# Second self-attention of a two-block model: 32x32 block transposes on VectorE and a gather by ScalarE's transfers in place of TensorE transposes

## The chip, the cores and the metric

One core of a Trainium2 chip runs the whole program in one launch. The metric is the device time of one execution in microseconds. All matrices are fp32. The large products are made on TensorE as three fp32r products of a high and a low part (high times high, high times low, low times high), so that every weight tile is first rounded to its high part and then has its rest taken.

## What is computed

Two blocks run one after the other on x of 512 tokens by 1024 features, each of two layers. In both layers of the second block one of three branches is a self-attention with 8 query heads and 2 key/value heads of 64 features, over all 512 tokens:

```python
q = rmsnorm(q.reshape(B, L, 8, 64), qn); k = rmsnorm(k.reshape(B, L, 2, 64), kn)
q, k = apply_rope_2(q, cos, sin), apply_rope_2(k, cos, sin)
s = jnp.einsum("bkgqd,bktd->bkgqt", qblk, k) * 64 ** -0.5     # per block of 128 queries
p = jax.nn.softmax(s, axis=-1)
o = jnp.einsum("bkgqt,bktd->bkgqd", p, v)                     # then @ w_br_attn, gated
```

The other two branches of such a layer are a long convolution and a gated linear attention. Their products, the gates' and the branches' output products stand between the pieces of this attention in the program.

## The kernel before

The program is a list of units (`order_of_work`), each a product with its weights or a small step, and every engine walks the same list and takes from each unit its own part. Engines meet through semaphores. So the order of the list is the order of each engine's queue, and an instruction that waits holds up all that stands behind it on its engine. Where several lists of units are merged, a string of digits (`PICKS`) says which list gives the next unit; they were fixed beforehand.

**Weights.** SyncE loads weight tiles of 512 or 256 KB into three raw buffers (`next_raw`, L2542), ScalarE rounds them to the high part (`next_halves`, L1327), GpSimd takes the rest (`next_rest`, L1710), and TensorE multiplies (L929 to L931). There are three split buffers, and the part of tile w + 2 stands in the unit of tile w. A product with 8 slices of 128 rows has 24 matmuls (the units `q`, `gate`, `gvtok`), one with 4 slices has 12 (`by`).

**The attention of a layer** goes over c = 0..3 (pairs of query heads, one pair in each c, hh = 0, 1) and in it over i = 0..3 (128 queries each):

- `sc` (L1098): for hh = 0, 1 a fp32 product of 64x128 queries and 64x512 keys into a score bank. There are three score banks, taken in turn (S0, S1, O).
- VectorE takes the row's maximum of each bank (L2088) and scales it (L2092). ScalarE exponentiates both (L1515), with the sum of each row, from the score banks into PB, which holds two i.
- `tr` (L994): TensorE transposes the eight 128x128 pieces of PB into banks T0 and T1. VectorE copies T0 (L2118) and ScalarE T1 (L1535) into PTB, in which keys lie on partitions.
- VectorE inverts the sums (L2104) and spreads them over VF (L2111).
- `pbc` (L994): four transposes of VF; ScalarE copies them back to VF (L1519).
- `pv` (L1125): after the fourth i, eight fp32 products of V (128x64) with PTB (128x512) into bank O, in two halves of the array. `bsplit` multiplies by VF (L1961) and splits the result for the branch's product (L1447, L1796).

Queries are rotated with eight small transfers on SyncE's queue for each c (QB<-RXB). In a layer `tr` occurs 16 times and `pv` 4 times. Behind the last `pv` the gated linear attention begins: `gfront` (L1213), `gscan` with its exponentials on ScalarE (L1582 to L1586), and `gvtok`, which takes the four banks S0, S1, T0, T1.

```python
score_bank: return (S0, S1)[hh] if ab == "a" else (S0, S1, O)[(2 * i + hh) % 3]
for hh in range(2):                                            # tr on TensorE
    b = take((T0, T1)[hh], (dve_done, act_done)[hh], ("pt", ab, l, c, i, hh))
    turn(b, [p[:, 128 * j:128 * j + 128] for j in range(nk)], nk, ...)
```

## Time and profile before

| | before |
|---|---|
| median of 3 runs | 3297.48 us (3294.96 to 3297.59) |
| span of the profiled execution | 3292.6 us |
| own time of the profiled execution | not given apart from its span; the median is 4.9 us above that span |
| busy: TensorE / VectorE / ScalarE / GpSimd | 3269.6 / 1593.0 / 1305.8 / 1569.4 us |
| chain that ended last, share of TensorE | 93% |
| first layer's attention, from its first `sc` to the next stage | about 1337 to 1463 us |
| second layer's | about 2430 to 2557 us |

"Busy" of an engine is the time in which at least one of its instructions ran. Matmuls overlap in the records: one that is shown as 0.39 us can start 0.23 us after the one before it. So the cost of a matmul is read as the distance between starts. A row with x8 stands for eight merged instructions. A fp32 product is recorded as two, so that `sc` shows x4 and `pv` x16.

### The profile page before, as it was taken

The numbers are of one execution on the slowest core, as the hardware profiler recorded it, in microseconds if no ns is written. First come the engines' busy times: TensorE is split into PE (matmuls) and PEld (weight loads), VectorE is DVE, ScalarE is ACT, GpSimd is POOL, SyncE is SP. The second block draws the span as 40 slices with busy tenths as digits, with TensorE's granted clock in tenths as the row PEclk, the third lists the DMA queues.
The fourth block names the chain that finished last, engine by engine and source line by source line (L and its number), as shares of the span: only waits on it lengthen the run. The fifth ranks groups of instructions, "written<-read, shape, count | busy, mean of one in ns | idle before, by whom it ended". The sixth has DMA issues, their size and how long they took to land.

```text
span 3292.6 us, 40481 instructions
## 1 busy us (share of the span) xinstructions
PE 3269.6 (99%) x15412; PEld 2574.7 (78%) x15412; DVE 1593.0 (48%) x2704; ACT 1305.8 (40%) x2016; POOL 1569.4 (48%) x1224
## 2 busy tenths in 40 slices
PE   9999999999999999999999999999999999999999
PEld 7788778787778767767888888887676788888887
DVE  4566433537543679654555321227875455442020
ACT  4333643333463322554446322232245444543231
POOL 4554344545334553224463565646332445546473
PEclk9999999999999999999999999999999999999999
DMA  4222224323323523212352433333231235333322
GB/s 160 96 87 91 82 84 152 111 87 93 100 74 96 180 78 125 87 55 87 120 179 94 135 118 96 105 123 122 90 119 55 68 103 190 117 124 128 96 90 96
DMA packets 127546, 353.40 MB, mean 107 GB/s; under 512 B 16622, under 2 KB 17198, under 8 KB 127352
## 3 DMA queue, kind: packets, MB, share of 16 engines
q1 hardware_dynamic: 127352, 350.82, 33.5%
q8 instruction: 122, 2.00, 0.2%
q14 instruction: 72, 0.59, 0.1%
HBM read 316.02 MB, written 25.30 MB: 104 GB/s over the span
## 4 chain that ended last, share of the span: by engine, by line
PE 93%; DVE 3%; ACT 1%; issue 1%; POOL 1%; SPq 1%; DMA 1%; DVEq 0%; ACTq 0%
PE B L929 27%; PE B L931 27%; PE B L930 27%; PE B L994 2%; PE B L1098 1%; PE B L1125 1%; PE B L1144 1%; PE B L1186 1%; PE B L1194 1%; PE B L1175 1%; PE B L1069 1%; POOL WSP L1710 1%; PE B L1060 1%; PE B L1180 0%; SPq L2533 0%
## 5 line engine op out<-in xcount | busy, mean ns | idle before, releaser
L1710 POOL TENSOR_TENSOR WSP<-WRAW,WSP 128x512 fp32r<-128x512 f32 x1036 | 1357.5, 1331 | 1512.4 <-ACT WSP L1327 1511.9
L929 PE MATMUL B<-H,WSP 128*128 128x512 f32 x2496 | 992.7, 398 | 3.0 <-POOL WSP L1710 3.0
L931 PE MATMUL B<-H,WSP 128*128 128x512 f32 x2496 | 972.4, 390 | 0.0
L930 PE MATMUL B<-H,WSP 128*128 128x512 f32 x2496 | 971.9, 389 | 0.0
L1327 ACT ACTIVATE WSP<-WRAW 128x1024 fp32r<-128x1024 f32 (+1 forms) x567 | 555.6, 984 | 664.4 <-PE B L931 525.0
L929 PEld LDWEIGHTS B<-H,WSP 128*128 128x128 f32 x2496 | 468.7, 188 | 122.0 <-issue 21.9
L930 PEld LDWEIGHTS B<-H,WSP 128*128 128x128 f32 x2496 | 468.9, 188 | 100.6 <-issue 7.0
L931 PEld LDWEIGHTS B<-H,WSP 128*128 128x128 f32 x2496 | 468.5, 188 | 99.2
L1793 DVE TENSOR_TENSOR B<-B,RN 128x512 f32<-128x512 f32 x194 | 135.0, 697 | 422.2 <-PE B L931 405.9
L929 PE MATMUL B<-YM,WSP 128*128 128x512 f32 x512 | 199.4, 389 | 0.0
L931 PE MATMUL B<-YM,WSP 128*128 128x512 f32 x512 | 199.2, 389 | 0.0
L930 PE MATMUL B<-YM,WSP 128*128 128x512 f32 x512 | 199.2, 389 | 0.0
L2516 DVE SCALAR_TENSOR_TENSOR MR<-B,RN 128x512 f32<-128x512 f32 x64 | 44.3, 692 | 249.8 <-PE B L931 249.7
L2524 DVE TENSOR_TENSOR XN<-B,XN 128x512 f32<-128x512 f32 x32 | 22.1, 692 | 294.1 <-PE B L931 294.1
L1781 POOL TENSOR_TENSOR MR<-MR 128x512 f32<-128x512 f32 x64 | 88.6, 1384 | 91.3 <-DVE MR L2516 89.1
L929 PEld LDWEIGHTS B<-YM,WSP 128*128 128x128 f32 x512 | 96.1, 188 | 21.4 <-DVE XN L2524 1.6
L931 PEld LDWEIGHTS B<-YM,WSP 128*128 128x128 f32 x512 | 96.1, 188 | 20.0
L930 PEld LDWEIGHTS B<-YM,WSP 128*128 128x128 f32 x512 | 96.1, 188 | 19.9
L1347 ACT ACTIVATE GA<-B 128x512 f32<-128x512 f32 x48 | 28.7, 599 | 202.1 <-DVE B L1793 202.1
L929 PE MATMUL B<-YAC,WSP 128*128 128x512 f32 x256 | 103.9, 406 | 0.0
L930 PE MATMUL B<-YAC,WSP 128*128 128x512 f32 x256 | 101.4, 396 | 0.0
L931 PE MATMUL B<-YAC,WSP 128*128 128x512 f32 x256 | 101.3, 396 | 0.0
(454 smaller groups left out, 4876.9 us busy)
## 6 DMA issues: line engine op xcount, KB each, us to landing
WRAW<-in_wb SPq DMA_DIRECT2D x318, 512.0 KB, 3.6
WRAW<-in_wa SPq DMA_DIRECT2D x153, 512.0 KB, 3.6
WRAW<-in_wa SPq DMA_DIRECT2D x50, 256.0 KB, 2.6
WRAW<-in_wb SPq DMA_DIRECT2D x48, 256.0 KB, 2.8
parked<-HYT SPq DMA_DIRECT2D x24, 256.0 KB, 2.2
QA<-RXA SPq DMA_DIRECT2D x64, 64.0 KB, 2.0
xs<-PA SPq DMA_DIRECT2D x16, 256.0 KB, 4.4
WIN<-in_win SPq DMA_DIRECT2D x16, 256.0 KB, 3.8
```

The source lines that it names most:

```text
L929: e.matmul(o, L[0], R[0], start=first, stop=False)
L930: e.matmul(o, L[0], R[1], start=False, stop=False)
L931: return e.matmul(o, L[1], R[0], start=False, stop=last)
L994: x = e.transpose(b[:, 128 * i:128 * i + 128], src[i], eye)
L1060: e.matmul(b[:, 0:n], QA[half, c % 2, 128 * i:128 * i + 128], KA[half, 1, 0:n], start=True, stop=True).then_inc(*mm_done.up(("idx", l, c, ...
L1069: x = e.matmul(b[:, 8 * n + 2 * i:8 * n + 2 * i + 2], sq[:, 128 * i:128 * i + 128], pair[:, ::64], start=True, stop=True)
L1098: e.matmul(b[:, 0:n], q, kk, start=True, stop=True).then_inc(*mm_done.up(("sc", ab, l, c, i, hh)))
L1327: e.activation(WSP[:, i % NSP, 0, 0:n * cols], WRAW[:, i % NRAW, 0:n * cols], ACT.Copy).then_inc(*hi_done.up(i))
L1710: x = e.tensor_tensor(WSP[:, i % NSP, 1, c:c + CUT], WRAW[:, i % NRAW, c:c + CUT], WSP[:, i % NSP, 0, c:c + CUT].bitcast(fp32), ALU.subtract)
L1781: e.tensor_tensor(t, t, t, ALU.mult).then_inc(*pool_done.up((k, *a)))
L1793: e.tensor_tensor(pj(u)[:, :], pj(u)[:, :], RN[:, :], ALU.mult).then_inc(*dve_done.up(("scaled", u.pj)))
L2516: e.scalar_tensor_tensor(MR[:, c % 4, :], pj(u)[:, :], 0.0, RN[:, :], ALU.max, ALU.mult).then_inc(*dve_done.up(("pj", u.pj), (k, *a)))
```

## The change

In both layers of the second block:

- The unit `tr` goes. In its place stands `blocks`: VectorE transposes PB in blocks of 32x32 within its partitions' quarters (STREAM_TRANSPOSE, two of 128x512 for each i) into a new buffer BLK, then inverts and spreads the sums as before. The copies to PTB from T0 and T1 go too.
- After the fourth i a new unit `gather` on ScalarE's queue issues eight transfers of 256 KB. Each takes 32 partitions of BLK (2 KB rows, four to a partition) and lays them on the 128 partitions of PTB. `blocks` of the next c waits for them before it writes BLK, and `pv` waits for them.
- `pv` reads PTB and writes the bank in runs of 32 columns, since blocks of 32 keys and queries lie in another order. V's tokens are reordered to match where V is made (unit `vs`).
- Score banks are four (S0, S1, T0, T1), no longer three. VF gets a second buffer.
- The order of units: the scores of the next c, a query product and one product more stand ahead of `pv`; the last `pv` of a layer stands behind two `gvtok` units of the next stage. The digit strings and the place of a few gates and branch products are altered to fit.

What each engine's queue looks like is shown at three places, all in the first layer, c = 0.

TensorE, end of c = 0. Before (PB are the exponentials, VF the spread factors, PTB the transposed exponentials):

```order
L994 MATMUL B<-CST,PB 128x128 [waits s_act_done,s_dve_done]
L994 MATMUL B<-CST,PB 128x128 x3
L994 MATMUL B<-CST,PB 128x128 [waits s_act_done]
L994 MATMUL B<-CST,PB 128x128 x3
L1098 MATMUL B<-KB,QB 128x512 x2
L994 MATMUL B<-CST,VF 128x128 [waits s_dve_done]
L994 MATMUL B<-CST,VF 128x128 x3
L1125 MATMUL B<-PTB,VB 64x512 [waits s_act_done,s_dve_done]
L1125 MATMUL B<-PTB,VB 64x512 x7
```

and now:

```order
L936 MATMUL B<-YBC,WSP 128x512
L937 MATMUL B<-YBC,WSP 128x512
L1000 MATMUL B<-CST,VF 128x128 [waits s_dve_done,s_act_done]
L1000 MATMUL B<-CST,VF 128x128 x3
L1126 MATMUL B<-PTB,VB 64x4x4x32 [waits s_gathered]
L1126 MATMUL B<-PTB,VB 64x4x4x32 x7
```

The eight transposes are gone, a branch product (YBC) stands ahead of `pbc` and `pv`, and `pv` waits for the gather's semaphore.

VectorE, the end of c = 0 now (L1819 scales a gate's bank):

```order
L2117 TENSOR_REDUCE SM<-B 128x1 [waits s_mm_done] x2
L2121 SCALAR_TENSOR_TENSOR SM<-SM 128x2 [waits s_dve_done]
L1819 TENSOR_TENSOR B<-B,RN 128x512 [waits s_mm_done]
L2136 STREAM_TRANSPOSE BLK<-PB 128x16x32 [waits s_act_done,s_dve_done]
L2136 STREAM_TRANSPOSE BLK<-PB 128x16x32 [waits s_act_done]
L2138 RECIPROCAL SM<-SM 128x2
L2145 COPY VF<-SM 128x128 [waits s_dve_done]
L2136 STREAM_TRANSPOSE BLK<-PB 128x16x32 [waits s_act_done] x2
```

The transposes of the third and the fourth i stand behind the scaling of a gate, which waits for that gate's product on TensorE.

ScalarE, the end of c = 0 now (GB is that gate, WSP the high part of a weight tile, RXB the next queries):

```order
L1342 ACTIVATE WSP<-WRAW 128x512 [waits s_mm_done,s_raw2,s_act_done]
L1362 ACTIVATE GB<-B 128x512 [waits s_dve_done]
L1562 DMA PTB<-BLK 128x1x512 [waits s_landed36,s_dve_done,s_landed35,s_act_done]
L1562 DMA PTB<-BLK 128x1x512 x7
L1530 ACTIVATE PB,SM<-B,SM 128x512 [waits s_dve_done]
L1530 ACTIVATE PB,SM<-B,SM 128x512
L1342 ACTIVATE WSP<-WRAW 128x512 [waits s_mm_done,s_raw0,s_act_done]
L1365 ACTIVATE RXB<-B 128x512 [waits s_dve_done]
```

Eight transfers are issued between a gate and the next exponentials; before, ScalarE issued none, and a copy to PTB stood after each i.

```diff
@@ -510,24 +510,24 @@
         main = head
         for c in range(4):
             nxt = qc(c + 1) if c < 3 else []
-            for i in range(4):
-                if i or not c:
-                    main.append(Unit("sc", "b", l, c, i, s=True))
-                if i:
-                    main.append(Unit("tr", "b", l, c, i - 1, t=True))
-                main += nxt[:1] if i == 0 else nxt[1:] if i == 1 else []
-            main.append(Unit("tr", "b", l, c, 3, t=True))
+            if not c:
+                main += [Unit("sc", "b", l, 0, 0, s=True), *nxt[:1], Unit("sc", "b", l, 0, 1, s=True)]
+            main += [Unit("blocks", l, c, 0), *nxt[1:], Unit("sc", "b", l, c, 2, s=True), Unit("blocks", l, c, 1),
+                     Unit("sc", "b", l, c, 3, s=True), Unit("blocks", l, c, 2), Unit("blocks", l, c, 3), Unit("gather", l, c)]
             if c < 3:
-                main.append(Unit("sc", "b", l, c + 1, 0, s=True))
-            main += [Unit("pbc", l, c, pj=True), Unit("pv", "b", l, c, o=True), Unit("bsplit", l, c)]
+                main += [Unit("sc", "b", l, c + 1, 0, s=True), *qc(c + 2)[:1 if c < 2 else 0], Unit("sc", "b", l, c + 1, 1, s=True)]
+            values = [Unit("pbc", l, c, pj=True), Unit("pv", "b", l, c, o=True), Unit("bsplit", l, c)]
+            main += values if c < 3 else []
...
+        branch = branch[:1] + [u for c in range(7) for u in (branch[2 * c + 2], branch[2 * c + 1])] + branch[15:]
         out += merged(tokens, filters, parts, main, gates, [u for u in second if u.kind == "by"],
-                      [u for u in second if u.kind == "gate"] + branch[:1], [proj("lr", l, src=H, w=[(*B, "lr", 0)])],
+                      [u for u in second if u.kind == "gate"] + branch[:2], [proj("lr", l, src=H, w=[(*B, "lr", 0)])],
...
+        tokens = [Unit("gvtok", l, j, src=H, w=[(*B, "gv", j)], s=(j == 0), t=(j == 0)) for j in range(4)]
+        main += tokens[:2] + values + tokens[2:]
...
-        VF, RXB, PB, PTB, GB = at(35, "VF", 1), at(31, "RXB", 4), at(36, "PB", 4), at(40, "PTB", 8), at(61, "GB", 3)
+        VF, RXB, PB, PTB, GB = at(35, "VF", 1), at(31, "RXB", 4), at(36, "PB", 4), at(48, "PTB", 8), at(61, "GB", 3)
+        BLK, VF1 = at(40, "BLK", 8), at(56, "VF1", 1)
...
-            return (S0, S1)[hh] if ab == "a" else (S0, S1, O)[(2 * i + hh) % 3]
+            return (S0, S1)[hh] if ab == "a" else (S0, S1, T0, T1)[(2 * i + hh) % 4]
+
+        def spread_tile(c):
+
+            return (VF, VF1)[c % 2][:, 0, :]
...
+                elif k == "pv" and a[0] == "b":
+                    ab, l, c = a
+                    b = take(O, dve_done, ("bsplit", l, c))
+                    w.wait_ge(gathered, ("gather", l, c))
+                    w.wait_ge(act_done, ("vturn", l))
+                    for j in range(4):
+                        for hh in range(2):
+                            v = VB[:, 0, 128 * j + 64 * (c // 2):128 * j + 64 * (c // 2) + 64]
+                            x = e.matmul(b[64 * hh:64 * hh + 64, :].rearrange("p (i r q) -> p r i q", i=4, r=4), v,
+                                         PTB[:, 4 * hh:4 * hh + 4, 128 * j:128 * j + 128].rearrange("p r (i q) -> p r i q", i=4),
+                                         start=j == 0, stop=j == 3)
+                    x.then_inc(*mm_done.up(("pv", *a)))
...
-                        w.wait_ge(mm_done, ("tr", ab, l, *back, 1))
+                        w.wait_ge(dve_done, ("blocks", l, *back, 1))
...
+                elif k == "gather":
+                    l, c = a
+                    if c:
+                        w.wait_ge(mm_done, ("pv", "b", l, c - 1))
+                    else:
+                        for n in (5, 6, 7):
+                            w.wait_ge(landed, ("parked", l, n))
+                    w.wait_ge(dve_done, ("blocks", l, c, 3, 1))
+                    for hh in range(2):
+                        for q in range(4):
+                            e.dma_start(PTB[:, 4 * hh + q, :], BLK[32 * q:32 * q + 32, 4 * hh:4 * hh + 4, :]).then_inc(
+                                *gathered.up((k, *a)))
...
-                    by_factor(u, VF[:, 0, :]).then_inc(*dve_done.up(("pj", u.pj), (k, *a)))
+                    by_gathered = [x.rearrange("p (b n) -> p b n", b=4) for x in (pj(u)[:, :], RN[:, :])]
+                    w.wait_ge(mm_done, (k, *a))
+                    e.tensor_tensor(VF[:, 0, :].rearrange("p (n b) -> p b n", b=4), *by_gathered, ALU.mult).then_inc(
+                        *dve_done.up(("pj", u.pj), (k, *a)))
...
+                elif k == "blocks":
+                    l, c, i = a
+                    m = SM[:, 6 + i, :]
+                    if i == 0 and c:
+                        w.wait_ge(gathered, ("gather", l, c - 1))
+                    for hh in range(2):
+                        w.wait_ge(act_done, ("exp", "b", l, c, i, hh))
+                        o = BLK[:, 4 * hh:4 * hh + 4, :].rearrange("p s (j i q) -> p i s j q", j=4, i=4)[:, i]
+                        e.transpose(o.rearrange("p s j q -> p (s j) q"), PB[:, 2 * (i % 2) + hh, :]).then_inc(
+                            *dve_done.up(("blocks", l, c, i, hh)))
+                    e.reciprocal(m[:, 6:8], m[:, 4:6]).then_inc(*dve_done.up(("rsum", "b", l, c, i)))
+                    if c > 1:
+                        w.wait_ge(dve_done, ("shared", l, c - 2))
+                    elif c == 0:
+                        w.wait_ge(mm_done, ("vturn", l))
+                    w.wait_ge(dve_done, ("rsum", "b", l, c, i))
+                    wide = spread_tile(c)[:, 128 * i:128 * i + 128].rearrange("p (n f) -> p n f", f=64)
+                    e.tensor_copy(wide, m[:, 6:8].unsqueeze(2).to_broadcast([128, 2, 64])).then_inc(*dve_done.up(("share", l, c, i)))
```

## Rows read from the trace of the kernel before

**Rows 1.** The page: span, and busy time of each engine.
```profile
span 3292.6 us, 40481 instructions
PE 3269.6 (99%) x15412; PEld 2574.7 (78%) x15412; DVE 1593.0 (48%) x2704; ACT 1305.8 (40%) x2016; POOL 1569.4 (48%) x1224
```
**Rows 2.** Waits of TensorE, whole run: us in total, times, longest.
```profile
PE B L994 <- DVE PTB L2118: 1.0, 2, 0.5
PE B L1125 <- ACT PTB L1535: 0.5, 2, 0.2
```
**Rows 3.** Instructions of `sc` (L1098): idle before them, whole run, us and times.
```profile
  ACT PB L1515: 11.4, 14
```
**Rows 4.** Groups by line, 1336 to 1464 us: busy us, mean ns, idle before.
```profile
L994 PE MATMUL B<-CST,PB 128*128 128x128 f32 x128 | 17.2, 277 | 0.5 <-DVE PTB L2118 0.5
L1125 PE MATMUL B<-PTB,VB 128*64 128x512 f32 x64 | 14.6, 598 | 0.2 <-ACT PTB L1535 0.2
...
L2088 DVE TENSOR_REDUCE SM<-B 128x1 f32<-128x512 f32 x32 | 20.9, 684 | 3.3 <-PE B L1098 3.1
L2118 DVE COPY PTB<-B 128x512 f32<-128x512 f32 x16 | 10.9, 682 | 0.0
...
L1515 ACT ACTIVATE PB<-B,SM 128x512 f32<-128x512 f32 x32 | 24.6, 775 | 30.0 <-DVE SM L2092 20.3 <-DVE SM L2104 9.6
L1535 ACT ACTIVATE PTB<-B 128x512 f32<-128x512 f32 x16 | 9.5, 594 | 0.5 <-PE B L994 0.5
```
**Rows 5.** Timeline of TensorE, first layer: start us, duration us, line, tiles.
```profile
1349.29 1.13 PE L1098 MATMUL B<-KB,QB 64*128 64x512 f32 x4
1350.35 1.09 PE L994 MATMUL B<-CST,PB 128*128 128x128 f32 x8
1351.20 0.48 PE L929 MATMUL B<-YBC,WSP 128*128 128x512 f32 x1
...
1370.57 1.04 PE L994 MATMUL B<-CST,PB 128*128 128x128 f32 x8
1371.53 1.13 PE L1098 MATMUL B<-KB,QB 64*128 64x512 f32 x4
...
1373.45 3.65 PE L1125 MATMUL B<-PTB,VB 128*64 128x512 f32 x16
1377.03 0.50 PE L929 MATMUL B<-H,WSP 128*128 128x512 f32 x1
...
1382.70 1.13 PE L1098 MATMUL B<-KB,QB 64*128 64x512 f32 x4
...
1385.58 1.98 PE L1098 MATMUL B<-KB,QB 64*128 64x512 f32 x4
1387.49 1.09 PE L994 MATMUL B<-CST,PB 128*128 128x128 f32 x8
```
**Rows 6.** Timeline of SyncE's queue: transfers issued one after another.
```profile
1351.97 0.59 SPq L2533 DMA_DIRECT2D QB<-RXB  x1
1352.60 0.59 SPq L2562 DMA_DIRECT2D QB<-RXB  x1
```
**Rows 7.** Transfers: count, KB each, median us from issue to landing.
```profile
parked<-HYT SPq DMA_DIRECT2D x24, 256.0 KB, 2.2
```
**Rows 8.** Windows: length, busy of PE, PEld, DVE, ACT, POOL, clock, DMA share, GB/s.
```profile
10.00:15.00 5.00, 5.00 (x23) 3.89 (x22) 3.91 (x6) 3.68 (x6) 0.00 (x0) 1.00 1.04 412
...
1336.45:1463.47 127.02, 124.63 (x589) 82.37 (x587) 66.22 (x135) 67.52 (x128) 31.63 (x25) 1.00 0.23 71
```
**Rows 9.** Timeline of ScalarE: first exponential of the `sc` that began at 1365.25.
```profile
1368.30 0.78 ACT L1515 ACTIVATE PB<-B,SM 128x512 f32<-128x512 f32 x1 [1.93 <-DVE SM L2104]
```
**Rows 10.** Timelines, start of the next stage: ScalarE's `gscan`, then TensorE.
```profile
1467.26 0.63 ACT L1582 ACTIVATE ES<-LG 128x512 f32<-128x512 f32 x1 [2.22 <-DVE LG L2316]
...
1475.76 1.99 ACT L1327 ACTIVATE WSP<-WRAW 128x1024 fp32r<-128x1024 f32 x2
...
1481.00 0.50 PE L929 MATMUL B<-WSP,H 128*128 128x512 f32 x1 [0.96 <-POOL WSP L1710]
```

More of the change, by code:

```diff
@@ L529, in mix_second @@
         main += [Unit("gscan", l, 0)]
-        main += [Unit("gvtok", l, j, src=H, w=[(*B, "gv", j)], s=(j == 0), t=(j == 0)) for j in range(4)]
+        tokens = [Unit("gvtok", l, j, src=H, w=[(*B, "gv", j)], s=(j == 0), t=(j == 0)) for j in range(4)]
+        main += tokens[:2] + values + tokens[2:]
         for hp in range(2):
@@ L545, in mix_second @@
         n = [(u.kind, *u.a) for u in keys].index(("xkss", l, 1))
-        out += merged(main, branch[1:], keys[:n], picks=PICKS["gla1" if l else "gla"])
+        out += merged(main, branch[2:], keys[:n], picks=PICKS["gla1" if l else "gla"])
         last = [Unit("gld", l)]
@@ L1111, in tensor @@
                         w.wait_ge(dve_done, ("share", *a, i))
-                    turn(b, [VF[:, 0, 128 * i:128 * i + 128] for i in range(4)], 4, (k, *a))
+                    turn(b, [spread_tile(a[1])[:, 128 * i:128 * i + 128] for i in range(4)], 4, (k, *a))
+                elif k == "pv" and a[0] == "b":
[10 more added lines that the diff above has]
+                    x.then_inc(*mm_done.up(("pv", *a)))
@@ L1113, in tensor @@
                 elif k == "pv":
                     ab, l, c = a
-                    PT = PTA if ab == "a" else PTB
-                    b = take(O, dve_done, ("lo", "YB", ("a", l), c) if ab == "a" else ("bsplit", l, c))
+                    b = take(O, dve_done, ("lo", "YB", ("a", l), c))
                     w.wait_ge(dve_done, ("pt", ab, l, c, 3, 0))
                     w.wait_ge(act_done, ("pt", ab, l, c, 3, 1))
-                    w.wait_ge(act_done, ("tok", "vtok", l, 3) if ab == "a" else ("vturn", l))
+                    w.wait_ge(act_done, ("tok", "vtok", l, 3))
@@ L1120, in tensor @@
                     for j in range(4):
-                        q0 = 128 * j if ab == "a" else 0
+                        q0 = 128 * j
                         for hh in range(2):
-                            v = VA4[:, j, 128 * c + 64 * hh:128 * c + 64 * hh + 64] if ab == "a" else \
-                                VB[:, 0, 128 * j + 64 * (c // 2):128 * j + 64 * (c // 2) + 64]
-                            x = e.matmul(b[64 * hh:64 * hh + 64, q0:512], v, PT[:, 4 * hh + j, q0:512], start=j == 0, stop=j == 3)
+                            v = VA4[:, j, 128 * c + 64 * hh:128 * c + 64 * hh + 64]
+                            x = e.matmul(b[64 * hh:64 * hh + 64, q0:512], v, PTA[:, 4 * hh + j, q0:512], start=j == 0, stop=j == 3)
@@ L1529, in scalar @@
                     ab, l, c, i = a
-                    nk = i + 1 if ab == "a" else 4
-                    PT = PTA if ab == "a" else PTB
+                    nk = i + 1
                     if i == 0 and c:
@@ L1960, in vector @@
                     w.wait_ge(mm_done, ("pv", "b", l, c))
-                    e.tensor_tensor(banks[O][:, :], banks[O][:, :], VF[:, 0, :], ALU.mult).then_inc(*dve_done.up(("shared", l, c)))
+                    e.tensor_tensor(banks[O][:, :], banks[O][:, :], spread_tile(c), ALU.mult).then_inc(*dve_done.up(("shared", l, c)))
                     w.wait_ge(dve_done, ("shared", l, c))
@@ L2098, in vector @@
                     e.reciprocal(m[:, 6:8], m[:, 4:6]).then_inc(*dve_done.up(("rsum", ab, l, c, i)))
+                elif k == "blocks":
[16 more added lines that the diff above has]
+                    e.tensor_copy(wide, m[:, 6:8].unsqueeze(2).to_broadcast([128, 2, 64])).then_inc(*dve_done.up(("share", l, c, i)))
                 elif k == "tr":
                     ab, l, c, i = a
-                    if ab == "b":
-                        m = SM[:, 6 + i, :]
-                        w.wait_ge(act_done, ("exp", ab, l, c, i, 1))
-                        e.reciprocal(m[:, 6:8], m[:, 4:6]).then_inc(*dve_done.up(("rsum", ab, l, c, i)))
-                        if c:
-                            w.wait_ge(dve_done, ("shared", l, c - 1))
-                        else:
-                            w.wait_ge(mm_done, ("vturn", l))
-                        w.wait_ge(dve_done, ("rsum", ab, l, c, i))
-                        wide = VF[:, 0, 128 * i:128 * i + 128].rearrange("p (n f) -> p n f", f=64)
-                        e.tensor_copy(wide, m[:, 6:8].unsqueeze(2).to_broadcast([128, 2, 64])).then_inc(
-                            *dve_done.up(("share", l, c, i)))
-                    nk = i + 1 if ab == "a" else 4
-                    PT = PTA if ab == "a" else PTB
+                    nk = i + 1
                     if i == 0 and c:
@@ L2713, in sync @@
             w.value(s_out, 16 * stores)
+            w.value(*gathered.turn())
             for i in range(len(landed.sems)):
```

22 lines of the change are left out of this document (11 added, 11 removed).

## The prediction, made before the changed kernel ran

> **What bounds the kernel now.** I read the page's busy times first [rows 1]: TensorE has an instruction running in 3269.6 of 3292.6 us, no other engine in more than 1593.0. So a microsecond off TensorE's queue counts in full, and work of the others costs only what TensorE waits for. The granted clock is 1.00 through the attention [rows 8], TensorE's higher level of 2.4 GHz. Next the list of who waited for whom [rows 2], then the waits by line [rows 3], since a stalled `sc` is busy in the records and does not show as idle: `sc` waited 11.4 us in 14 places for exponentials. Then the groups by line [rows 4], for the counts and durations, and the timeline of TensorE [rows 5], in which distances between starts give what a unit costs. From it I take: a lone `sc` 1.06 us (1349.29 to 1350.35); `tr` 0.85 us ahead of a product (1350.35 to 1351.20) and 0.96 ahead of `sc` (1370.57 to 1371.53); `pv` 3.58 (1373.45 to 1377.03); 24 matmuls of a product 5.67 (1377.03 to 1382.70), so 12 of them 2.8; a stalled `sc` 1.91 (1385.58 to 1387.49).
>
> **TensorE: what goes.** The first layer has 128 recorded transposes of PB [rows 4], 16 `tr` units; two layers have 32. At 0.90 us, between the two distances above, that is 28.8 us. Where `tr` stood between a product and `sc`, `sc` now pays the change of kind itself; I take 0.5 us off for the few such places: **28.3 us**.
>
> **TensorE: the waits that go.** With three score banks and PB freed by TensorE, `sc` waits for exponentials. Four banks taken in turn give each pair the time of one `sc` more, and the new order puts a product of 2.8 or 5.67 us between nearly all of them. I take the 11.4 us as gone [rows 3], with them the 1.0 and 0.5 us for the copies to PTB [rows 2]: **12.9 us**. Bounds: nothing, if other waits take their place one for one; 12.9 is the whole of it.
>
> **VectorE and ScalarE.** VectorE loses 32 copies of 682 ns and gets 64 block transposes [rows 4]. No such instruction is in this trace. Its nearest row is the copy of the same 128x512, 0.68 us; a reduction of the same shape takes 0.684. I take 0.68 and keep 1.36, two cycles an element, as the other end; below the copy I see no reason to go. So VectorE gets 11 us more in a layer, on 66.2 of 127.0 us busy [rows 8]: 61%, off the path except for the last transposes ahead of a gather. ScalarE loses 16 copies of 0.594 us in a layer, 9.5 us [rows 4], and gets 32 issues. None was issued there before; SyncE's queue issues one each 0.63 us (1351.97 to 1352.60) [rows 6], with 0.4 to 1.0 as bounds. Eight take 5.0 us, 20 in a layer: net 10.5 more on 67.5, 61% too. What stands behind the issue on ScalarE is the next exponentials, one weight tile's high part, and the query's squares. In the plan two tiles are ready ahead, 5.67 us each or 2.8, so this cover holds except in the fourth c (below). The strided write of V into VF happens once a layer, hidden by the next product.
>
> **The length of a gather** decides the rest. It moves 8 x 256 KB, 2.1 MB. A transfer of this size lands 2.2 us after its issue [rows 7], of which 0.6 is its data at the best rate that a window shows, 412 GB/s [rows 8]; so 1.6 is fixed. Lower end: 5.0 of issue less the last one's own 0.6, plus 2.2, say 7.0 us. That needs the best rate. But each transfer reads only 32 of 128 partitions, and they come in order, quarter by quarter. If a quarter of the partitions gave a quarter of the rate (103 GB/s), it would be 20.4 + 1.6 = 22 us. Weight loads take another 71 GB/s here, a share of 0.23. I take half of the best rate, 206 GB/s, since the small transfers of a few partitions show no such slowness as the low end asks: 10.2 + 1.6 = **11.8 us** from first issue to landing.
>
> The Trainium skill (SBUF — State Buffer, Door 1: The DMA port swizzle) says that transfer bandwidth goes by how many of 16 ports the partitions reach, and that 32 partitions reach 8, with 189 GB/s measured at 1 MiB; by it alone the data would take 11.1 us. No row here shows a transfer of that kind large enough to agree or not.
>
> **What `pv` has in hand.** I count from the start of a c's last `sc`. The first exponential starts 3.05 us after it (1365.25, [rows 9]), the second 0.77 later, done at 4.6; a last pair of transposes ends at 5.5 or so if VectorE is free.
> - c = 0: VectorE's last four transposes stand behind the gate's scaling, which waits for its product: 1.06 + 5.67 + 0.7 = 7.4, four transposes and small ones 3.3: the gather starts at 10.7. TensorE comes to `pv` after `sc`, gate, `sc`, query, `sc`, branch, `pbc`: 3 x 1.06 + 2 x 5.67 + 2.8 + 0.6 = 17.9. In hand 7.2 us, wait 4.6.
> - c = 1: the next query's squares and copy stand on ScalarE behind the issue of the gather, its eight small transfers behind them (8 x 0.63 and 2 more to land), so VectorE's three rotations and the maxima behind them come late; the last transposes end at 7.3, `pv` at 17.9, in hand 10.6. The wait of c = 0 lets VectorE catch up by 0.8: in hand 11.4, wait 0.4.
> - c = 2: gather at 6.2, that is 5.5 and 0.7 for the sums' small steps; ahead of `pv` stand 3 `sc`, 2.8, 5.67 and 0.6: 12.3. In hand 6.1, wait 5.7.
> - c = 3: two `sc` and a gate follow each other. From the end of `pv` VectorE has the result's two steps and their wait on ScalarE (2.0), three `blocks` (2.0 each), two pairs of maxima (1.4 each), the gate's scaling (0.7) and the last transposes (1.4): 12.9, less 1.06 for the `sc` ahead, so the gather starts at about 12.2 with a step or two of waiting; `gvtok` has to wait 1.5 for the last exponentials to free its banks. `pv` comes at 22. In hand 9.8, wait 2.0. Then ScalarE starts `gscan` only after the issue; before, that took 8.5 us to the next weight tile (1467.26 to 1475.76) and cost TensorE 0.96 us [rows 10]. Now the third `gvtok` would come 2.5 us late; the wait of `pv` covers 2.0 of it, 0.5 stays.
>
> Per layer 4.6 + 0.4 + 5.7 + 2.0 + 1.5 + 0.5 = 14.7, two layers 29.4, less the 1.9 that the old start of the next stage cost: **27.5 us** of new waits.
>
> **`pv`'s runs of 32 columns**: 128 recorded matmuls, 28.6 us by the distance above. I take no change; the recorded products all read runs of 128 or more, so the other end is half as much again, 14 us.
>
> **Sum.** 28.3 + 12.9 - 27.5 = 13.7 us less. On the profiled execution 3292.6 becomes 3278.9 of span; on the median, 4.9 us above it, 3297.5 becomes **3284**. About 0.2%, 6.6 us, is what a measurement of this kernel tells from no change.
>
> **Rivals.**
> 1. *The gather keeps pace with its issue*, 7.0 us. Speaking for it: 412 GB/s were reached beside other work, and weight loads fill only 0.23 of the engines in this stretch [rows 8]. Then only c = 2 waits, 0.9, and the fourth c 1.5 + 2.5: 4.9 a layer, 9.8 less 1.9 is 7.9. Gain 28.3 + 12.9 - 7.9 = 33.3: **3264**. Chance 0.30.
> 2. *Slower: the gathers are longer still.* The place is TensorE ahead of each `pv`. From 11.8 us on every microsecond of a gather counts eight times, so 13.7 us of gain last until 13.5 us, a rate of 176 GB/s. At 16 us, 146 GB/s, with weight loads in the same engines, it is 8 x 4.2 = 34 less 14: 20 slower, **3317**; at the low end of 22 us, 3365. An issue on ScalarE of over 1.5 us each does the same. Against it: weight loads use only 0.23 here. Chance 0.13.
> 3. *The block transposes cost double.* Each gather starts later by 2 or 4 times 0.68, so about 8 us a layer less what c = 1 has in hand: 13 in all, **3297**, no change. The Trainium skill (VectorE: DVE Perf Modes, The three transpose paths) gives 311 ns for 128x128 in bf16 on VectorE, and its rules for authors send a 128x128 transpose to TensorE. Four times that would be 1.24 us for 128x512, near this rival. No row here shows it. Chance 0.12.
> 4. *`pv` pays for its short runs*, 14 us: **3298**, no change. Chance 0.05.
>
> **How the numbers follow.** The forecast has 0.40. Its own spread (issues of 0.4 to 1.0 us, old waits that don't all go, a few tenths in each c) is some 9 us to both sides, so 3275 to 3293; nearly all of it is faster by over 6.6 us, 0.06 is not. Faster: 0.34 + 0.30 + 0.04 of rivals 3 and 4 at smaller prices = 0.68. Slower: 0.13 and 0.03 of the others: 0.16. Same: 0.16. The range has to take in rival 1 with its own 4 us below, 3260, and on the far side rivals 3 and 4 and the near part of rival 2, 3304; left out are the far part of rival 2 and gains over 37 us, under 2 in 10.
>
> **What would show it.** No TensorE transposes of PB, 256 fewer. Block transposes at 0.6 to 0.75 us. Issues on ScalarE 0.6 us apart, eight times eight. First issue to the `pv` behind it: landing after 11 to 13 us says the forecast, 7 says rival 1, over 13.5 rival 2. Waits of `pv` for the transfers of 4 to 6 us in c = 0 and c = 2, little in c = 1. Waits of `sc` for exponentials close to nothing. `pv` at 3.6 us from start to next start; at 5 us rival 4. I am wrong as a whole if `sc` still waits some 10 us, or if weight tiles are late behind the issues in more than the fourth c.

## The result

| | before | after |
|---|---|---|
| median | 3296.84 us (3294.96 to 3297.59, 4 runs) | 3311.66 us (3310.07 to 3316.01, 4 runs) |
| ratio, 95% interval | | 1.0047 [1.0036, 1.0059] |
| profiled execution: span | 3292.6 us | 3314.2 us (own time 3316.01) |

The change makes the kernel 14.8 us **slower**. The prediction was 3284, 13 us faster, with 3260 to 3304 as its range: wrong in sign, and outside the range. Between the two profiled spans lie 21.6 us: that of before is 4.2 us under its median, that of after 2.5 us over its own (it is the slowest of its four). Each sum on the trace is made against the 21.6.

### The profile page after: what moved, and what is told of

Its sections match the earlier page's. It is cut to its first block, busy times and chain, and to the rows that moved or that the text cites. A ratio compares the mean times of both kernels' runs of the same rounds, so it can differ in the third digit from the quotient of the medians.

```text
span 3314.2 us, 40025 instructions
## 1 busy us (share of the span) xinstructions
PE 3250.8 (98%) x15156; PEld 2556.3 (77%) x15156; DVE 1607.1 (48%) x2736; ACT 1288.2 (39%) x1986; POOL 1570.0 (47%) x1224
## 4 chain that ended last, share of the span: by engine, by line
PE 89%; DVE 5%; ACTq 2%; ACT 1%; DMA 1%; issue 1%; POOL 0%; SPq 0%; DVEq 0%
PE B L935 26%; PE B L937 26%; PE B L936 26%; ACTq L1562 2%; PE B L1000 1%; PE B L1104 1%; PE B L1126 1%; PE B L1159 1%; PE B L1201 1%; PE B L1209 1%; PE B L1190 1%; DVE BLK L2136 1%; DMA PTB<-BLK 1%; PE B L1075 1%; PE B L1066 1%
## 5 line engine op out<-in xcount | busy, mean ns | idle before, releaser
L935 PE MATMUL B<-H,WSP 128*128 128x512 f32 x2496 | 994.8, 399 | 4.6 <-POOL WSP L1736 4.6
L935 PEld LDWEIGHTS B<-H,WSP 128*128 128x128 f32 x2496 | 469.3, 188 | 133.8 <-issue 27.0
L1819 DVE TENSOR_TENSOR B<-B,RN 128x512 f32<-128x512 f32 x194 | 134.9, 697 | 404.8 <-PE B L937 388.5
L935 PE MATMUL B<-YM,WSP 128*128 128x512 f32 x512 | 199.4, 389 | 0.0
L935 PEld LDWEIGHTS B<-YM,WSP 128*128 128x128 f32 x512 | 96.1, 188 | 21.4 <-DVE XN L2558 1.6
L935 PE MATMUL B<-YAC,WSP 128*128 128x512 f32 x256 | 103.2, 403 | 0.0
```

The costliest lines, as they stand in the source:

```text
L935: e.matmul(o, L[0], R[0], start=first, stop=False)
L1819: e.tensor_tensor(pj(u)[:, :], pj(u)[:, :], RN[:, :], ALU.mult).then_inc(*dve_done.up(("scaled", u.pj)))
```

## The profile of the changed kernel

The page, beside [rows 1]: TensorE has 256 matmuls fewer in a span 21.6 us longer. Its busy time fell by 18.8 us only, though the transposes alone were 28.3 and old waits that counted as busy come on top. And outside its busy time it stands 63.4 us, where it stood 23.0.

```profile
span 3314.2 us, 40025 instructions
...
PE 3250.8 (98%) x15156; PEld 2556.3 (77%) x15156; DVE 1607.1 (48%) x2736; ACT 1288.2 (39%) x1986; POOL 1570.0 (47%) x1224
```

Who waited for whom on TensorE in the whole run (total us, times, longest). First before, the lines that matter now:

```profile
PE B L929 <- POOL WSP L1710: 6.6, 8, 1.1
...
PE B L1278 <- DVE KSQ L2451: 0.8, 1, 0.8
```

and after, where L935 is a product's matmul (L929 before), L1126 `pv`, L1293 the units `xkss` (a sum of squares of the cross attention's keys, ahead of which a `by` product stood before), L1269 the unit `gout` of the linear attention:

```profile
PE B L1126 <- DMA PTB<-BLK: 26.3, 8, 5.7
PE B L935 <- POOL WSP L1736: 16.0, 9, 5.9
PE B L1293 <- DVE KSQ L2485: 5.3, 2, 3.4
PE B L1000 <- ACT PA L1541: 3.4, 3, 1.8
PE B L1269 <- DVE SS L2436: 2.8, 2, 1.4
```

Four waits grew: `pv` for the gather by 26.3, weight tiles by 9.4, and in the stage behind `xkss` by 4.5 for KSQ and `gout` by 2.8 for SS, for which it did not wait before. The waits of [rows 2] for PTB are gone with the copies. (The fourth line is code of the first block, 2.6 us before.)

The groups by line in the first layer's attention, 1336 to 1484 us, beside [rows 4] (busy us, mean ns, idle before):

```profile
L1530 ACT ACTIVATE PB<-B,SM 128x512 f32<-128x512 f32 x32 | 24.6, 776 | 51.6 <-DVE SM L2121 22.8 <-issue 19.2 <-DVE MSB L2170 9.7
L2136 DVE STREAM_TRANSPOSE BLK<-PB 128x512 f32<-128x512 f32 x32 | 20.7, 685 | 0.0
...
L1126 PE MATMUL B<-PTB,VB 128*64 128x512 f32 x62 | 20.1, 806 | 13.7 <-DMA PTB<-BLK 13.7
L1104 PE MATMUL B<-KB,QB 64*128 64x512 f32 x64 | 17.5, 634 | 0.0
```

A block transpose takes 685 ns, as the copy did. But a matmul of `pv` has a mean of 806 ns where it had 598, with the same number of columns. The timeline of TensorE says why (start, duration, line, in brackets the idle time before and what ended it). The four `pv` of the first layer:

```profile
1382.38 6.63 PE L1126 MATMUL B<-PTB,VB 128*64 128x512 f32 x16 [4.51 <-DMA PTB<-BLK]
1418.91 3.65 PE L1126 MATMUL B<-PTB,VB 128*64 128x512 f32 x16 [1.36 <-DMA PTB<-BLK]
1450.82 6.54 PE L1126 MATMUL B<-PTB,VB 128*64 128x512 f32 x16 [5.64 <-DMA PTB<-BLK]
1481.25 3.65 PE L1126 MATMUL B<-PTB,VB 128*64 128x512 f32 x16 [2.14 <-DMA PTB<-BLK]
```

The same sixteen matmuls take 3.65 us behind waits of 1.36 and 2.14 us, as in [rows 5], and 6.6 behind waits of 4.51 and 5.64. In the second layer they take 5.35 us behind a wait of 4.20, 3.65 behind 0.24, 5.00 behind 5.73, and 5.35 behind one of only 2.44:

```profile
2582.19 5.35 PE L1126 MATMUL B<-PTB,VB 128*64 128x512 f32 x16 [2.44 <-DMA PTB<-BLK]
```

So a slow `pv` stands behind each long wait, but also behind a shorter one. Against 3.65 us each, the five that take longer lose 10.6 us. In windows (length; busy of PE, PEld, DVE, ACT, POOL; granted clock; DMA share; GB/s) the first `pv`, the attention of the first layer and that of the second:

```profile
1382.38:1389.00 6.62, 6.62 (x17) 1.77 (x17) 0.00 (x0) 2.54 (x6) 2.49 (x2) 0.54 0.28 65
...
1336.50:1484.00 147.50, 132.62 (x552) 85.77 (x552) 83.58 (x166) 67.24 (x124) 37.34 (x29) 0.95 0.46 120
2443.00:2589.00 146.00, 130.06 (x544) 83.51 (x542) 81.98 (x165) 69.76 (x126) 39.24 (x30) 0.96 0.46 121
```

The clock granted to the slow `pv` is 0.54, nearly all of it the lower level of 1.2 GHz; over the stage it is 0.95 where [rows 8] had 1.00. The Trainium skill (TensorE: Matmul & The Clock Gate, HAM oscillation — how this bites in real kernels) describes this pattern, a wait for a transfer followed by matmuls at half rate; the trace agrees, and nothing in my sum stood for it.

The gather of c = 3 on ScalarE's timeline, with what is queued behind it, and the first product that comes late for it on TensorE's:

```profile
1468.97 9.09 ACTq L1562 DMA_DIRECT2D PTB<-BLK  x8
1478.11 0.63 ACT L1608 ACTIVATE ES<-LG 128x512 f32<-128x512 f32 x1 [9.42 <-issue]
...
1485.65 1.99 ACT L1342 ACTIVATE WSP<-WRAW 128x1024 fp32r<-128x1024 f32 x2
```

```profile
1490.85 0.80 PE L935 MATMUL B<-WSP,H 128*128 128x512 f32 x1 [5.95 <-POOL WSP L1736]
1491.45 0.63 PE L936 MATMUL B<-WSP,H 128*128 128x512 f32 x1
...
1494.58 0.39 PE L935 MATMUL B<-WSP,H 128*128 128x512 f32 x1
1494.81 0.39 PE L936 MATMUL B<-WSP,H 128*128 128x512 f32 x1
```

Eight issues hold ScalarE for 9.09 us, not 5.0. The weight tile is late by 5.95 us where I had 0.5 left, and behind that wait a matmul of a product costs 0.43 us from start to start until 1494, 0.23 after. The issues by themselves (ns min/median/max), and from issue to landing:

```profile
L1562 ACTq DMA_DIRECT2D PTB<-BLK x64: 550/1018/2304, 1369.8 to 2577.6; - x64
...
DMA to landing us min/median/max: 3.6/4.7/5.8
```

The first two issues of each gather take 0.55 to 0.65 us, the third 1.2 to 1.4, the fourth 1.2 to 1.9, and the last four between 0.6 and 2.3, unevenly. From the first issue (1369.85) to `pv` (1382.38) it is 12.5 us, over all eight gathers 12.0 to 12.6, of which the data take 10.2 to 11.0 from the first packet to the last.

The last place lies 150 us behind the attention. `xkss` in the first layer, before and after, each from TensorE's timeline:

```profile
1625.93 0.67 PE L1278 MATMUL B<-KSQ,CST 128*128 128x256 f32 x2 [0.78 <-DVE KSQ L2451]
```

```profile
1638.77 1.19 PE L1293 MATMUL B<-KSQ,CST 128*128 128x256 f32 x2 [3.39 <-DVE KSQ L2485]
1639.40 0.78 PE L935 MATMUL B<-MN,WSP 128*128 128x256 f32 x1
```

It waits 2.6 us longer, and what follows runs at the lower clock again. In the order of units a `by` product of 12 matmuls (2.8 us) stood between `gback` and `xkss`. The change used one gate more inside the attention, and the strings of digits that were written to fit have that last `by` earlier.

**The balance of the two spans.** -28.3 (transposes) - 12.9 (old waits) + 26.3 (`pv`) + 9.4 (weight tiles) + 4.5 (KSQ) + 2.8 (SS) + 1.3 (waits for exponentials that are left) is +3.1; 18.5 us are not in it. TensorE's clock stood at the lower level for 65 us of this execution, before for 10. In 56 of the 65 us TensorE was busy, and half of that, 28, is lost; before it was 5. These 23 us are enough for the 18.5, and 4.5 more, so one of the other terms is too high by about that much; which one is open. Whether the waits are the cause of these stretches had to be tried.

## Experiments

All times are medians; the kernel before ran beside each group and gave 3296.5, 3296.2 and 3296.8. The changed kernel has 3311.7, from one group of four runs. Runs e1, e3, e5 and e9 were executed 11 times each, the others 4 or 5 times; the runs of one kernel lie 3 to 12 us apart, so a difference of 4 us between two of the short ones is not clear of noise. Runs e1 to e12 are told by what they test.

### Does a wait cost twice? (e1)

```diff
 b = take(O, dve_done, ("bsplit", l, c))
+for n in range((16, 4, 20, 8)[c]):
+    e.matmul(b[:, :], H[:, 0, 0, 0:128], H[:, 0, 0, :], start=True, stop=True)
 w.wait_ge(gathered, ("gather", l, c))
```

> Changed kernel, and ahead of each pv's wait for the gather TensorE runs 16, 4, 20 and 8 extra matmuls (c = 0 to 3) into the bank that pv overwrites; nothing else changes. The extra matmuls stand in a wait that is there anyway (4.5, 1.4, 5.6 and 2.1 us in the first layer), so they should cost nothing. Theory (the wait lets the granted clock fall, and pv and the products behind it then run at half speed): clock 1.00 through both attentions, pv 3.65 us from start to start in c = 0 and c = 2 where it was 6.6, and 10 to 16 us less than the changed kernel: 3296 to 3302. Rival (the half-speed stretches come by themselves and would be there without the waits): they stay, and the time is 3311 to 3316, more by what the extra matmuls overrun.

Measured: **3299.2** (1.0010 [1.0002, 1.0019] of before), 12.5 us less than the changed kernel, by adding 96 matmuls. The two slow `pv` of the first layer:

```profile
1378.53 3.65 PE L1128 MATMUL B<-PTB,VB 128*64 128x512 f32 x16 [0.56 <-DMA PTB<-BLK]
...
1443.98 3.65 PE L1128 MATMUL B<-PTB,VB 128*64 128x512 f32 x16 [1.56 <-DMA PTB<-BLK]
```

The windows of the two attentions:

```profile
1336.50:1475.00 138.50, 134.84 (x587) 90.08 (x585) 79.43 (x160) 66.67 (x122) 36.75 (x29) 1.00 0.49 128
2433.00:2571.00 138.00, 135.77 (x584) 91.09 (x584) 78.25 (x161) 67.59 (x124) 36.73 (x28) 0.99 0.49 128
```

`pv` starts 12.2 us after the first issue (1366.29), so the gather is as long as it was and TensorE as late for it; what is different is the clock, and with it 12.5 us. All eight `pv` take 3.65 us. The expectation of clock 1.00 held in the first layer and nearly in the second, where one stretch at the lower clock stayed, near 2553 us and with no wait over 0.9 us beside it. So the idle waits of `pv` cause the half-speed stretches at `pv`, and there the rival falls. The stretches behind the weight tile of c = 3 (waits of 5.6 and 4.2 us) and behind `xkss` are still there, as are three far ahead of the attention that the kernel before has too; the lower level stands for 31 us of this execution, where it stood for 65.

### Who pays for slow issues? (e3)

The block of eight `dma_start` and its waits, taken out of ScalarE's program and put into SyncE's at the same unit:

```diff
         def scalar(e):
...
-                elif k == "gather":
-                    l, c = a
...
-                            e.dma_start(PTB[:, 4 * hh + q, :], BLK[32 * q:32 * q + 32, 4 * hh:4 * hh + 4, :]).then_inc(
...
         def sync(e):
...
+                elif k == "gather":
+                    l, c = a
...
+                            e.dma_start(PTB[:, 4 * hh + q, :], BLK[32 * q:32 * q + 32, 4 * hh:4 * hh + 4, :]).then_inc(
```

> Changed kernel with the gather's eight transfers issued from SyncE's queue in place of ScalarE's; waits for the same things. Theory (an issue holds ScalarE 1.1 us in the mean, 8.9 a gather, and so makes weight tiles late: 16.0 us of TensorE's waits for the rests of weight tiles, 6.6 before): those waits fall to 7 or so, the waits of pv stay at 26, 8 to 14 us less than the changed kernel with what the clock gives back: 3298 to 3304. Rival (SyncE's weight loads then stand behind the issues and their wait, and come as late as the tiles did): waits for weight tiles stay at 16 or grow, 3311 or more.

Measured: **3296.3** (0.9999 [0.9990, 1.0008]), 15.4 us less: somewhat more than the 8 to 14 expected. Its waits and its issues:

```profile
PE B L1126 <- DMA PTB<-BLK: 29.6, 8, 6.1
PE B L935 <- POOL WSP L1724: 6.4, 7, 1.4
```

```profile
L2724 SPq DMA_DIRECT2D PTB<-BLK x64: 555/959/2339, 1370.2 to 2574.1; - x64
```

Weight tiles are back at 6.4, as before the change. SyncE's issues take as long as ScalarE's did (959 ns against 1018 in the middle), so it is not the issuing engine that makes them slow. Nor is it the 256 KB alone: SyncE's transfers of 256 KB to `parked`, which do not follow each other so closely, take 0.33 us each to issue in both kernels. That the transfers still under way hold an issue back fits both, and that the first two of each gather are short; no run tests it by itself. SyncE can afford it: ScalarE waits for loaded weights 121.5 us in the whole run, 119.0 in the changed kernel and 121.2 before.

### Where did xkss's cover go? (e2, e8, e9)

e2 moved one digit in each string:

```diff
-    "gla": "000000000010000001100001000011000000001000000001101000110010120222202002200202022",
+    "gla": "000000000000000011000010000110000000010000000011010001100101202222020022002012022",
```

> Changed kernel with one digit of the order moved in each layer: the branch product that stood behind the second gvtok's stage goes, all branch products and gates there stand one place later, and the last one (12 matmuls) stands again between gback and xkss, as before the change. Theory (the wait of xkss for KSQ, 3.4 and 2.0 us, and the half-speed stretch behind it are a loss of cover by reordering, and no work of the attention): the wait is under 1 us again, no half clock there, 8 to 12 us less than the changed kernel: 3300 to 3304. Rival (the wait only moves to the place from which the cover was taken, or the drift there is run to run): 3309 to 3313.

Measured: **3316.0** (1.0062 [1.0049, 1.0074]), 4.3 us more than the changed kernel; the rival was right. The wait for KSQ did fall to 0.9, and three others came:

```profile
PE B L1245 <- ACT ES L1632: 4.4, 2, 2.2
...
PE B L935 <- DVE SM L2441: 1.8, 1, 1.8
...
PE B L1245 <- DVE SS L2436: 1.4, 2, 0.8
```

`gstate` (L1245) waits for ES and SS: the product that I took, behind `gvtok`, and the shift of all the others by a place had covered it. e8 is e4 (below) with another choice: the last `by` back ahead of `xkss`, taken from in front of `gout`, with a gate and a `by` exchanged to make up for it.

> Kernel of e4 with the order at the end of the gated linear attention mended another way than in e2: the last branch product stands between gback and xkss again, and the gate ahead of it changes places with a branch product, so that gout keeps a product of 24 matmuls ahead of it as before the change. Theory (the wait of xkss for KSQ, 5.1 us in two layers, and the half-speed stretches behind it come from the lost cover): that wait under 1.5 us, no new wait over 1 us at gout, 7 to 12 us less than e4: 3262 to 3267. Rival (the cover is again taken from somewhere else, as in e2): 3272 or more.

Measured: **3276.5**, against 3274.2 of e4: no gain, the rival again. `gout` (L1271 here) now waits in its place:

```profile
PE B L1271 <- DVE SS L2441: 7.0, 2, 3.5
```

e9 is the changed kernel with the third choice, the `by` ahead of the second `gstate`, and the same exchange:

```diff
+        branch[-3], branch[-2] = branch[-2], branch[-3]
         out += merged(main, branch[2:], keys[:n], picks=PICKS["gla1" if l else "gla"])
...
-    "gla": "000000000010000001100001000011000000001000000001101000110010120222202002200202022",
+    "gla": "000000000010000001100001000011000000001000000001101000100101202222020022002012022",
```

> Changed kernel with its order at the end of the gated linear attention mended, now without loss at gout: the branch product between two stages of the state (ahead of the second gstate) is the one taken out, the last one stands again between gback and xkss, and a gate (24 matmuls) stands again ahead of gout. In e2 and e8 the wait only moved, to gstate and gout. Theory: the waits of xkss for KSQ (5.3 us) and of gout for SS (2.8 us) both fall under 1 us in sum, the half-speed stretches near 1645 and 2740 us go, 8 to 13 us less than the changed kernel: 3299 to 3304. Rival (whatever stands where, 2.8 us of cover are missing in this stage, since the change used one gate more in the attention): a new wait of 2 us or more at gstate or its neighbours, 3308 or more.

Measured: **3303.7** (1.0021 [1.0012, 1.0030]), 8.0 less. `xkss` and `gout`, from 8.1 us together, wait for KSQ 0.6 us in one place and not for SS at `gout` (`gstate` waits 2.1 for it), and there is no half-speed stretch behind. The theory wanted KSQ and SS together under 1 us; they are at 2.7, though each of the two waits at `gstate` is only about 1.0 us, and the time is in its range. So of the three places tried, one could spare a product and two could not; which it was came out of the list of waits of each try, not out of counting matmuls.

### All three together (e10)

> Changed kernel with the three things mended that my prediction left out, and nothing else: extra matmuls in the waits of pv (e1), issues from SyncE (e3), the order of e9. The waits of pv for the gather stay, 26 to 30 us. Theory (these three are the whole gap between 3284 and 3312): 3281 to 3289. Rival (something not found yet costs some us more): 3291 or more.

Measured: **3285.9** (0.9967 [0.9955, 0.9980]), 25.8 us less than the changed kernel and 10.9 less than before; the prediction was 3284. The theory holds. The waits of `pv` in its list are down to 4.1 us, but only because the 96 extra matmuls, some 22 us of them, stand in their place: from first issue to `pv` it is 12.3 to 12.8 us wherever `pv` still waits. Singly the three gave 12.5, 15.4 and 8.0, in sum 35.9, where together they give 25.8. They overlap; that each also takes away half-speed stretches that another would have is the likely reason (65 us at the lower level in the changed kernel, 31, 48 and 45 with one of them, 11 with all), but it is not shown apart.

### How fast can a gather be? (e5)

```diff
-for q in range(4):
+for q in (0, 2, 1, 3):
```

> Changed kernel; only the order of the eight transfers of a gather differs: quarters 0, 2, 1, 3 of the partitions for each hh in place of 0, 1, 2, 3. Theory A (a transfer that reads 32 partitions is bound by the eight ports they reach, quarters 0 and 1 reach the same eight, and two transfers in flight from quarters 0 and 2 use all sixteen): the data of a gather take 6 to 8 us in place of 10.2 to 11.0, the issues are held back less, pv waits fall from 26.3 to under 10 us, 12 to 25 us less than the changed kernel: 3287 to 3300. Rival B (transfers of one queue follow each other, or the limit is elsewhere, in the engines or at the writing side, which takes all 128 partitions in every transfer): nothing changes, 3309 to 3315.

Measured: **3300.5** (1.0013 [1.0004, 1.0022]), 11.2 less. But the gather changed little:

```profile
1365.16 7.98 ACTq L1562 DMA_DIRECT2D PTB<-BLK  x8
```

```profile
1376.46 3.65 PE L1126 MATMUL B<-PTB,VB 128*64 128x512 f32 x16 [3.26 <-DMA PTB<-BLK]
```

First issue to `pv` is 11.3 us here where it was 12.5, the issues take 8.0 in place of 8.9. Over the gathers that `pv` waits for, the mean is 11.4 us in place of 12.3, and the data take 8.8 to 10.0 in place of 10.2 to 11.0. The waits of `pv` fell from 26.3 to 19.8. Theory A, with 6 to 8 us of data, is wrong; that nothing changes is wrong too. The Trainium skill (SBUF — State Buffer, "Can I just issue two DMAs to hit both halves?") has two concurrent transfers on different halves only 6% faster than one; the trace, with 7%, is near that. Of the 11.2 us the waits of `pv` give 6.5, but weight tiles take 2.1 back (18.1 us, from 16.0). The rest fits the clock: behind the wait of c = 0, now 3.26 us, `pv` takes 3.65 us, and the lower level stands for 37 us of this execution where it stood for 65, though 10 of the 28 less lie ahead of the attention, where the edit changes nothing. The Trainium skill (SBUF — State Buffer, Door 1: The DMA port swizzle) gives 189 GB/s for 32 partitions, by which a gather's data would take 11.1 us (an estimate). The trace of the changed kernel, with 10.2 to 11.0, agrees; with quarters 0, 2, 1, 3 the data are faster than that.

### A gather in two halves (e4)

PTB and BLK are laid out by pairs of i; the first pair's four transfers (h = 0; 256 KB each, as before) stand in ScalarE's program at the `sc` of the fourth i, ahead of its exponentials, the second pair's (h = 1) at `gather`, and `pv` works in two halves of 256 columns:

```diff
+for r in range(4):
+    e.dma_start(PTB[:, 4 * h + r, :], BLK[32 * r:32 * r + 32, 4 * h:4 * h + 4, :]).then_inc(...)
-o = BLK[:, 4 * hh:4 * hh + 4, :].rearrange(...)[:, i]
+o = BLK[:, 4 * h:4 * h + 4, :].rearrange(...)[:, 2 * hh + i % 2]
```

> Changed kernel with each gather in two halves of four transfers of 256 KB: the first pair of i leaves as soon as its transposes are done, ahead of the last exponentials, the second pair as before; pv works in two halves of 256 columns, each behind its own gather (64 more matmuls recorded in two layers, same columns). Theory (pv waits because 2.1 MB leave after the last transposes; the transfers' rate is fixed at some 200 GB/s): the second half lands 5 to 6 us earlier, so the waits of pv fall from 26.3 to under 6 us in the whole run, the clock stays 1.00 in the attention, issues are held back less (0.63 to 0.8 us each): 25 to 35 us less than the changed kernel: 3277 to 3287, faster than before the change. Rival (the first half's issues hold the last exponentials back by as much as is won, or pv in halves of 256 columns costs over 1 us more each): 3300 or more.

Measured: **3274.2** (0.9931 [0.9917, 0.9944]), 37.5 less than the changed kernel, a little more than the 25 to 35 expected, and 22.3 less than before. `pv` does not wait for the gather at all any more. The head of the list of waits is now:

```profile
PE B L935 <- POOL WSP L1739: 6.6, 8, 1.2
PE B L935 <- ACT PB L1543: 6.4, 2, 3.3
PE B L1294 <- DVE KSQ L2489: 5.1, 2, 3.1
```

I had expected issues of 0.63 to 0.8 us each. That was wrong: four take 3.9 to 4.4 us, about as much for each as before. Those of the first half now stand ahead of the last exponentials, for which `gvtok` waits 3.3 and 3.1 us.

### Who should issue the halves? (e6, e7)

> Kernel of e4 (gather in two halves, 3274.2), with the first half's four transfers issued from SyncE's queue, the second half's from ScalarE. Theory (in e4 the first half's issues, 4.2 us, hold back the last exponentials, for which gvtok waits 3.3 us in each layer at their banks, with a half-speed stretch of 3.4 to 6.8 us behind it): gvtok's wait falls below 1.5 us, 6 to 12 us less than e4: 3262 to 3268. Rival (SyncE's wait for the second pair of transposes holds weight loads back, new waits for weight tiles): 3272 or more.

Measured: **3266.2** (0.9906 [0.9892, 0.9921]), 7.9 less than e4. The wait for exponentials fell from 6.4 to 2.2 in two, as the theory has it, though waits for weight tiles rose from 6.6 to 9.5.

> Kernel of e4 with both halves issued from SyncE's queue. Theory: as e6, and the second half's 4 us off ScalarE as well, so that waits for weight tiles behind it fall too: 3259 to 3267, no slower than e6. Rival (SyncE's queue, with twice the issues, its waits, the weight loads and the query's eight small transfers in it, is now late): weight tiles and query rotations late, slower than e6, 3268 or more.

Measured: **3267.3** (0.9907 [0.9894, 0.9921]), the same as e6 within 1.1 us. Waits for weight tiles fell from 9.5 to 5.1, as the theory has it, but those for exponentials are back at 5.2 (2.95 at 1451.51), and the two cancel.

### The best version (e11, e12)

> Kernel of e6 (two halves, first half's issues on SyncE, 3266.2) with the order of e9 and the quarters in the order 0, 2, 1, 3. Theory: KSQ's 4.8 us and SS's 2.8 us of waits and two half-speed stretches of 3.4 us go, the quarters give nothing more or up to 2 us at the start of the next stage: 3253 to 3260. Rival (gains don't add up, the wait moves on): 3263 or more.

Measured: **3262.3** (0.9894 [0.9879, 0.9909]), 4.0 less than e6, where 6 to 13 were expected. KSQ's wait fell from 4.8 to 0.7 us, but that for SS only moved, from 2.8 at `gout` to 2.1 at `gstate`, and weight tiles rose from 9.5 to 10.3: in part it is the rival, and less time was behind the waits than I had summed. No run took the order of quarters out again, so what each of the two gave here is open.

> As e11, and in the fourth c of each layer the second half's issues on SyncE too, so that ScalarE starts gscan at once. Theory (in e6 the weight tile of the second gvtok comes 1.8 and 2.6 us late behind these issues, with a half-speed stretch): 3 to 6 us less than e11. Rival (as in e7, where SyncE issued all: gvtok then waits 3.0 us for the last exponentials instead): the same as e11 within 2 us, or more.

Measured: **3258.2** (0.9883 [0.9870, 0.9897]): 4.1 less than e11, as the theory has it, though the runs of the two overlap (3255.6 to 3261.2 against 3259.4 to 3264.3), 38.6 less than before and 53.5 less than the changed kernel. Page and first waits:

```profile
span 3258.3 us, 40292 instructions
...
PE 3233.9 (99%) x15284; PEld 2556.7 (78%) x15284; DVE 1615.2 (50%) x2736; ACT 1287.7 (40%) x1986; POOL 1571.7 (48%) x1224
```

```profile
PE B L936 <- POOL WSP L1738: 9.0, 11, 1.2
PE B L1001 <- ACT PA L1553: 3.4, 3, 1.8
```

No wait of TensorE is over 1.8 us; weight tiles cost 2.4 us more than before the change, and `gstate` waits 2.1 for SS, which it did not.

## The prediction, step by step

**Right.** The transposes and their copies are gone, and block transposes take 0.68 us each (rival 3 falls). `pv` with runs of 32 columns takes 3.65 us where the clock is up (rival 4 falls). `sc` waits for exponentials no more than 0.7 us. From first issue to `pv` 12.5 us: the forecast had 11.8, rival 1 had 7.0, and break-even, had the rest held, was at 13.5. The waits of `pv` in the first layer were 4.5, 1.4, 5.6 and 2.1 us; I had 4.6, 0.4, 5.7 and 2.0. So what I took for the whole question was sized well. That it fits to a tenth is partly luck: in the first layer the gathers took 12.0 to 12.5 us, 0.2 to 0.7 more than forecast, while TensorE had 8.0, 11.0, 6.3 and 10.1 us in hand where I had 7.2, 11.4, 6.1 and 9.8. And half of the best rate was a choice between two ends, with little behind it. The sign "weight tiles late in more than the fourth c" did not come either: the long ones are both of the fourth c, only far later than forecast.

**Wrong, first: the price of a wait.** The sum charged each new wait at its own length, 27.5 us in all. Behind waits of 4.5 and 5.6 us, `pv` took 2.9 us more as well, 10.6 us more in all eight, and products behind other waits ran at half speed. No term stood for this. e1 puts the part that hangs on the waits of `pv` at 12.5 us, nearly half as much again as these waits. The rows read before could have warned only indirectly: the longest wait for a weight tile there was 1.1 us, so the clock at 1.00 [rows 8] was a fact of a kernel without long waits, and I carried it into one that has them.

**Wrong, second: 0.63 us for an issue on ScalarE.** I took SyncE's distance for small transfers [rows 6], with 1.0 as the upper bound. Those were 32 KB; these are 256 KB in close succession, and issues come 1.1 us apart in the mean. The step that failed is "eight take 5.0 us": they take 8.5 to 9.1. What I drew from it, that weight tiles are covered "except in the fourth c" and 0.5 us stays there, became 5.95 and 3.86 us in the two layers. With the clock's part, e3 puts it at 15.4 us. The text had "an issue on ScalarE of over 1.5 us each does the same" as part of rival 2, with a price for `pv` and none for the weight tiles: the right place, weighed for the wrong victim.

**Wrong, third: what is moved at a distance.** "The digit strings and the place of a few gates and branch products are altered to fit" was costed at nothing, without naming the work that hides it. The product that covered `xkss` was gone, and `gout` waited for SS: 4.5 and 2.8 us of waits and their clock, 8.0 by e9.

Together e10 is 3285.9 (five runs, 3280.5 to 3289.5), 1.9 us from the prediction, with the gathers as long as before. So these three are the gap, to within what the runs can tell. Not settled: how the 18.5 us beyond the balance divide among single stretches. Three of after's, and one of before's, lie near 900 to 945 us in code that is the same in both; e3, e4, e7 and e12 have three there too, the others one at most. That accounts for about 4 us that come and go from run to run, and it is in the profiled span of after.

## What to carry to other kernels

Price a new wait of some us on TensorE at its length plus what the matmuls behind it may lose at the lower clock (here 12.5 us beside 26.3 of waits), and split it or fill it; starting part of a transfer as soon as its part of the data exists was worth more here (37.5 us) than any mending of its rate. Ask for each large transfer issued from a compute engine how long its issue takes when others stand close ahead of it, and who waits for that engine meanwhile. When an order written by hand is refitted, look at the cover of every unit whose neighbour changed, however far from the change.

## What the hardware showed that I had not expected

- Adding 96 matmuls to a kernel bound by TensorE made it 12.5 us faster. Of the waits ahead of `pv`, all those of 4.20 to 6.35 us go with a slow `pv`. Below, the length alone does not tell: 3.26 and 2.99 us (e5) and 3.54 us (e2) left `pv` at 3.65 us, and 2.44 us (changed kernel) went with 5.35. A stretch at the lower clock also stands beside the wait of 1.96 us ahead of the second layer's `xkss`.
- Issues of 256 KB from one SBUF tile to another come equally slowly on ScalarE (median 1018 ns) and SyncE (959 ns), where SyncE's 32 KB ones took 0.59 and its 256 KB ones to `parked`, further apart, 0.33; the first two of a gather take about 0.6 us, the longer times come from the third on.
- Taking quarters of the partitions as 0, 2, 1, 3 shortens a gather of eight transfers from 12.3 to 11.4 us in the mean, a small but real gain for a change of one line.
